# Out projections of a one-core decoder layer: weight high parts against both parts of the activations in one 512-column matmul, two accumulators per tile, residual added two tiles at a time

## The reference

```
x = x + 0.5*g1 * ((silu(h@Wa) * (h@Wb)) @ w_ffn1_out)      # h = mod(rms(x)), D_FF = 5504
P = h @ w_in ; SSD mixer, S5 mixer ; merged = sig(ga)*(y_a@w_a) + sig(gb)*glu(y_b@w_b)
x = x + g2 * (merged @ w_out)                               # 2048 x 2048
x = x + 0.5*g3 * ((silu(h@Wa) * (h@Wb)) @ w_ffn2_out)
out = rms(x)*norm_final
```

## The kernel before, in words

| stage | phase | k tiles, k tiles per slab | ada slabs per body | after it |
|---|---|---|---|---|
| A | first FFN, out, first rows | 20: 4,4,3,3,3,3 | 4 | "in" stage |
| B | first FFN, out, last rows | 23: 4,4,4,4,4,3 | 8 | norm |
| C | w_out | 16: 4,4,4,4 | 4 | norm |
| D | second FFN, out, first rows | 20: 4,4,3,3,3,3 | 0 | "in" stage |
| E | second FFN, out, last rows | 23: 4,4,4,4,4,3 | 0 | final norm and output |

## Time and profile before

### The profile page before, as it was taken

How to read it: one execution, slowest core, us unless ns; L and a number is a source line. 1 busy time by engine, 2 the same in 40 slices (tenths; PEclk the granted TensorE clock), 3 DMA queues, 4 the chain that set the end, 5 groups by cost and what they waited for, 6 DMA issues and landing times. The chain is left out here.

```text
span 2542.8 us, 39831 instructions
## 1 busy us (share of the span) xinstructions
PE 2418.9 (95%) x16288; PEld 2200.0 (87%) x16288; DVE 1728.5 (68%) x2035; ACT 1034.6 (41%) x1109; POOL 222.5 (9%) x250
## 2 busy tenths in 40 slices
PE   5899999999999998889999979989999999999998
PEld 3478799887899998889999979989788899888998
DVE  3357877778778779798777767657767455444554
ACT  3233343333443454444444433433434344434443
POOL 2500413132133000000000000000000000000000
PEclk8899999999999999999999989999999999999999
DMA  9967777878877865454566658567678556655652
GB/s 332 360 244 275 267 272 259 302 256 297 273 263 269 308 233 166 158 190 167 166 209 215 213 177 281 181 212 269 233 248 308 185 183 199 194 187 176 195 176 99
DMA packets 296990, 584.58 MB, mean 230 GB/s; under 512 B 10324, under 2 KB 35412, under 8 KB 295316
## 3 DMA queue, kind: packets, MB, share of 16 engines
q1 hardware_dynamic: 291408, 559.98, 64.6%
q0 software_dynamic: 4144, 22.28, 2.5%
q10 hardware_dynamic: 1300, 0.35, 0.1%
HBM read 569.98 MB, written 12.58 MB: 229 GB/s over the span
## 5 line engine op out<-in xcount | busy, mean ns | idle before, releaser
L900 DVE TENSOR_TENSOR wlo<-raw,whi 128x1024 fp32r<-128x1024 f32 x800 | 984.6, 1272 | 591.4 <-ACT whi L524 580.2
L524 ACT ACTIVATE whi<-raw 128x1024 fp32r<-128x1024 f32 x800 | 803.6, 1052 | 1237.1 <-PE gps L296 1185.3
L296 PE MATMUL gps<-whi,hs 128*128 128x512 f32 (+1 forms) x2816 | 874.9, 389 | 25.1 <-DVE wlo L900 18.0
L296 PE MATMUL gps<-hs,whi 128*128 128x256 f32 x3584 | 662.9, 287 | 36.6 <-DVE hs L1448 14.9
L296 PEld LDWEIGHTS gps<-whi,hs 128*128 128x128 f32 x2816 | 532.0, 190 | 134.5 <-DVE wlo L900 22.4
L296 PEld LDWEIGHTS gps<-hs,whi 128*128 128x128 f32 x3584 | 564.2, 194 | 49.2 <-issue 29.0
L296 PE MATMUL gps<-wlo,hs 128*128 128x512 f32 (+1 forms) x1408 | 545.0, 387 | 0.0
L296 PE MATMUL gps<-hs,wlo 128*128 128x256 f32 x1792 | 509.8, 284 | 0.0
L296 PE MATMUL gps<-ffs,whi 128*128 128x256 f32 x2752 | 498.9, 284 | 5.3 <-DVE wlo L900 5.3
L296 PEld LDWEIGHTS gps<-ffs,whi 128*128 128x128 f32 x2752 | 429.1, 192 | 7.3 <-DVE wlo L900 6.9
L296 PE MATMUL gps<-ffs,wlo 128*128 128x256 f32 x1376 | 389.3, 283 | 0.0
(11 more groups left out here) (251 smaller groups left out, 1231.6 us busy)
## 6 DMA issues: line engine op xcount, KB each, us to landing
raw<-in_w_ffn_in_dram SPq DMA_DIRECT2D x160, 1024.0 KB
raw<-in_w_ada_dram SPq DMA_DIRECT2D x112, 1024.0 KB
raw<-in_w_in_dram SPq DMA_DIRECT2D x80, 1024.0 KB
raw<-in_w_ffn_out_dram SPq DMA_DIRECT2D x56, 1024.0 KB
pre<-in_w_ada_dram SPq DMA_DIRECT2D x32, 1024.0 KB, 13.8
raw<-in_w_ffn_out_dram SPq DMA_DIRECT2D x40, 768.0 KB
raw<-in_w_a_proj_dram SPq DMA_DIRECT2D x16, 1024.0 KB
raw<-in_w_b_glu_dram SPq DMA_DIRECT2D x32, 512.0 KB
```

The source lines that it names most:

```text
L296: return pe.matmul(out, lhsT, rhs, start=start, stop=stop, skip_group_check=True)
L524: act.activation(whi[:, mpos % SPLIT, h, :], raw[:, pos % RING, h, :], ACT.Copy).then_inc(hi_ready, 1)
L900: ins = dve.tensor_tensor(wlo[:, mpos % SPLIT, h, :], raw[:, pos % RING, h, :], whi[:, mpos % SPLIT, h, :].bitcast(F32), ALU.subtract)
```

## The change

In the five stages a tile j now has a whole bank: `wps` is the same memory as `gps` seen as four tiles of two 256-column accumulators. The weight's high part is multiplied with high and low activations in one matmul of 512 columns (both accumulators), the low part with the high activations in one of 256 columns (first accumulator). So three matmuls (768 columns, three weight loads) become two (768 columns, two weight loads). A group uses all four banks, so a group's first matmuls of tiles 0 and 2 wait until VectorE has read tiles 0,1 and 2,3 of the group before. VectorE adds each tile in two operations, the second after the first; tiles 0,1 as soon as the new `tiles_done` says so, tiles 2,3 when the group is done. The place in its queue moves up: right after the first slab of the next group (before: after the first two). The loops over bodies are written out on VectorE.

```diff
         gps = ctx.enter_context(nc.psum_tensor("gps", [P, 2, 4, S], F32))
         mps = ctx.enter_context(nc.psum_tensor("mps", [P, 4, 512], F32))
+        wps = gps[:, :, :, :].rearrange("p b (h w) s -> p (b h) w s", w=2)
...
             def squares(ph, n, q):
-                act.wait_ge(psum_free(n % 2), q)
+                act.wait_ge(psum_free(1), q)
...
                 elif ph.evac == "resid":
-                    ends = ph.norm is not None and 2 * i + g == 3
+                    n = 2 * i + g
+                    ends = ph.norm is not None and n == 3
+                    gate = hg[:, ph.gate, :]
+
+                    def add(j, part):
+                        t = 4 * n + j
+                        xt = xT[:, t, :]
+                        return dve.scalar_tensor_tensor(out=xt, in0=wps[:, j, part, :], scalar=gate[:, t:t + 1],
+                                                        in1=xt, op0=ALU.mult, op1=ALU.add)
+
+                    def add_both(tiles, count):
+                        for j in tiles:
+                            ins = add(j, 0)
+                        ins.then_inc(sem("x_step"), 1)
+                        dve.wait_ge(sem("x_step"), r.x + 2 * n + count)
+                        return [add(j, 1) for j in tiles]
+
+                    dve.wait_ge(sem("tiles_done"), r.t + n + 1)
+                    xs = add_both((0, 1), 1)
...
+                    xs[1].then_inc(psum_free(0), 1)
+                    if ends:
+                        dve.wait_ge(sem("tiles_done"), r.t + n + 2)
+                        add_both((2,), 2)[0].then_inc(sem("x_new"), 1)
+                        dve.wait_ge(slab_done, m_end)
+                        add_both((3,), 3)[0].then_inc(psum_free(1), 1)
                     else:
                         dve.wait_ge(slab_done, m_end)
-                    gate = hg[:, ph.gate, :]
-                    for j in range(4):
...
-                        ins = dve.scalar_tensor_tensor(out=xt, in0=out[:, j, :], scalar=gate[:, bass.ds(t, 1)],
-                                                       in1=xt, op0=ALU.mult, op1=ALU.add)
...
+                        add_both((2, 3), 2)[1].then_inc(psum_free(1), 1)
...
                                 next(side, None)
+                                if ph.wide and gg == 1 and s == 0:
+                                    evacuate(ph, i, 0, m0 + i * mper + ph.slabs, 0)
                         if g == 1:
...
+                            elif ph.wide:
+                                between = lambda: evacuate(ph, i, 1, m_end, 0)
...
+                def slab_wide(g, i, s, mp, k0):
+                    for j in range(4):
+                        if s == 0 and j % 2 == 0:
+                            pe.wait_ge(psum_free(j // 2), r.q + 2 * i + g)
+                        for k in range(ph.chunks[s]):
+                            hi = whi[:, mp % SPLIT, k, P * j:P * j + P]
+                            lo = wlo[:, mp % SPLIT, k, P * j:P * j + P]
+                            both = moving[:, k0 + k, :, :].rearrange("p w s -> p (w s)")
+                            mm(pe, wps[:, j, :, :].rearrange("p w s -> p (w s)"), hi, both, k0 + k == 0, False)
+                            ins = mm(pe, wps[:, j, 0, :], lo, moving[:, k0 + k, 0, :], False,
+                                     k0 + k == sum(ph.chunks) - 1)
+                        yield ins
...
-                                if ph.norm is not None and 2 * i + g == 3 and s == ph.slabs - 1 and j == 1:
-                                    ins.then_inc(sem("half_done"), 1)
+                                if ph.wide and s == ph.slabs - 1 and (
+                                        j == 1 or j == 2 and ph.ends and 2 * i + g == 3):
+                                    ins.then_inc(sem("tiles_done"), 1)
```

More of the change, by code:

```diff
@@ L85, in __init__ @@
         assert len(self.stream) % RING == 0 and n % SPLIT == 0
+        self.wide = evac == "resid"
+        self.rounds = (2 if self.wide else 1) * bodies
+        self.ends = 1 if norm is not None else 0
 def plan():
@@ L610, in evacuate @@
                     if ph.norm is not None and 2 * i + g == 3:
-                        last_squares(ph, q)
+                        last_squares(ph, r.q + 4)
                     return
@@ L703, in gemm @@
                 body(ph.bodies - 1, following)
-                r.q += ph.bodies
+                r.q += ph.rounds
                 r.p += {"pair": ph.bodies, "glu": 2 * ph.bodies}.get(ph.evac, 0)
@@ L951, in first_two @@
                     if s == 1 and between is not None:
-                        multiply(*between)
+                        between()
                     if i is None:
@@ L1010, in evacuate @@
-                    ins.then_inc(psum_free(b), 1)
+                        add_both((2, 3), 2)[1].then_inc(psum_free(1), 1)
                     if ph.norm == 3:
+                        for b in range(2):
+                            dve.wait_ge(psum_free(b), r.q + n + 1)
                         if ends:
-                            dve.wait_ge(sem("x_new"), 9)
-                        dve.wait_ge(psum_free(b), q)
+                            dve.wait_ge(sem("x_new"), 6)
                         for j in range(4):
-                            t = 8 * i + 4 * g + j
+                            t = 4 * n + j
@@ L1071, in body @@
                                 next(side, None)
+                                if ph.wide and gg == 1 and s == 0:
+                                    evacuate(ph, i, 0, m0 + i * mper + ph.slabs, 0)
                         if g == 1:
-                            between = (ph, m0 + i * mper + 2 * ph.slabs, r.q + i + 1) if ph.evac == "pair" else None
+                            m_end, between = m0 + i * mper + 2 * ph.slabs, None
+                            if ph.evac == "pair":
+                                between = lambda: multiply(ph, m_end, r.q + i + 1)
+                            elif ph.wide:
+                                between = lambda: evacuate(ph, i, 1, m_end, 0)
                             if nxt == "loop":
@@ L1082, in body @@
                                     pass
-                        evacuate(ph, i, g, m0 + i * mper + (g + 1) * ph.slabs, r.q + i + 1)
+                        if not ph.wide or g == 1 and (nxt is None or nxt != "loop" and ph.norm is not None):
+                            evacuate(ph, i, g, m0 + i * mper + (g + 1) * ph.slabs, r.q + i + 1)
                     if ph.ada:
                         ada_end(r.c + i * ph.ada + ph.ada - 1)
-                if ph.bodies > 1 and not ph.side and ph.norm is None:
+                if ph.bodies > 1 and not ph.side and not ph.wide:
                     if after_norm:
@@ L1095, in gemm @@
                 body(ph.bodies - 1, following)
-                r.q += ph.bodies
+                r.q += ph.rounds
+                if ph.wide:
+                    r.t, r.x = r.t + 4 + ph.ends, r.x + 8 + ph.ends
                 r.c += ph.ada * ph.bodies
@@ L1228, in early @@
             def early(ph, following):
-                first_two(following, between=(ph, 8, 1))
+                first_two(following, between=lambda: multiply(ph, 8, 1))
                 evacuate(ph, 0, 1, 8, 1)
@@ L1675, in body @@
                             pass
-                        else:
+                        elif not ph.wide:
                             pe.wait_ge(psum_free(g), r.q + i)
@@ L1686, in body @@
                                 pe.wait_ge(sem("prod_free"), ff_from[0] + (k0 + ph.chunks[s] + 3) // 4 + 1)
-                            if by_tile:
+                            if ph.wide:
+                                parts = slab_wide(g, i, s, mp, k0)
+                            elif by_tile:
                                 parts = (slab_pair_by_tile if ph.evac == "pair" else slab_plain_by_tile)(g, s, mp, k0)
```

18 lines of the change are left out of this document (6 added, 12 removed).

## The result

| | before | changed |
|---|---|---|
| median of the runs (6 and 6) | 2544.4 us | 2554.9 us |
| lowest to highest | 2543.8 to 2545.9 | 2553.5 to 2562.8 |
| profiled execution: time, span | 2544.55, 2542.8 | 2554.86, 2553.1 |
| ratio of times, 95% interval | | 1.0046 (1.0036 to 1.0057) |

What follows compares the result with a forecast made beforehand. TensorE was taken as the busy engine in all five stages, wholly in C, D and E. A 21.8 us gain against 29.9 of new waits gave +8.1, a median of 2553.6 us, range 2541 to 2561.

Steps and rivals of the forecast that it cites:

- What it removes: All five stages: three matmuls become two, a pair takes 0.3467 us for 0.3600; 1632 pairs save 21.8 us.
- its own sign: Stretches without waits: a pair starts every 0.347 us; the prediction is wrong if not within 0.345 to 0.349.
- its bounds: Time of a pair: 0.333 us if the removed weight load takes both fixed parts, 0.360 if nothing is gained.
- Waits at group ends: Ends of groups in A, B, D, E: TensorE waits for VectorE's adds behind a low part, typically losing 1.43 us.
- VectorE's queue: Doubled adds delay ada slabs and low parts, so TensorE waits: C 3.8, A 3.4, B 1.2 us; 8.4 together.
- the rival that these chains vanish: VectorE's chain is cheaper than counted; if its three terms vanish the sum is -0.3 us; chance 0.26.
- Ends of stages: Last adds of B, C and E finish later, by 2.2, 0.1 and 0.9 us.
- B's sum: Stage B: -4.9 saved, +2.9, +1.3, +1.2 and +2.2 added, net +2.7 us.
- the third rival: A cascade in A and B: waits delay low parts further or B's norm pause costs clock; +4 to +12 us; chance 0.06.
- The other side: One weight load less hides more: a pair below 0.3417 us makes the kernel faster, 2532 at the bound; chance 0.12.
- The one with no gain from merging: The pair costs what three matmuls cost, 0.36 us: +29.9, 2575.5 us; chance 0.03.

Runs made afterwards that it cites:

- narrow_two: The changed kernel with only the merging undone: three 256-column matmuls per tile and k tile, its layout, adds and waits kept; 2565.9 us, ratio 1.0086.
- last4: The changed kernel with slab sizes reordered so the last slab of each FFN output group has four k tiles, not three; 2545.9 us, ratio 1.0009.
- one_part: The changed kernel without the second accumulator's adds and without VectorE's wait for itself between the two adds; 2537.7 us, ratio 0.9977.
- the control: The kernel before with two slab-size tables reordered so the last slab has four k tiles; 2547.7 us, ratio 1.0016.
- ada_later: The changed kernel with the four ada slabs of each body in stage A one weight slab later; 2551.4 us, ratio 1.0029.
- grouped: The changed kernel with each tile's 512-column matmuls in a slab placed ahead of its 256-column ones; 2554.5 us, ratio 1.0043.
- orders: The changed kernel with four different orders of the 512- and 256-column matmuls tried in the groups of D and E; 2554.2 us.
- slab_runs: The changed kernel with all 12 or 16 512-column matmuls of a slab in D first, except in a group's last slab; 2552.7 us.

## Why the prediction was right, and where it was not

The table takes each stage to the first matmul of what follows (for E, to the end of the span). "Saved" after is 0.360 less the stage's mean pace, times its pairs; "added" is the net plus that.

| | saved, forecast / measured | added | net |
|---|---|---|---|
| A | 4.3 / 2.5 | 7.5 / 6.4 | +3.2 / +3.9 |
| B | 4.9 / 4.4 | 7.6 / 8.9 | +2.7 / +4.4 |
| C | 3.4 / 2.4 | 3.9 / 3.3 | +0.5 / +1.0 |
| D | 4.3 / 3.2 | 5.7 / 5.6 | +1.4 / +2.4 |
| E | 4.9 / 3.7 | 5.2 / 4.6 | +0.3 / +0.9 |
| sum | 21.8 / 16.2 | 29.9 / 28.8 | +8.1 / +12.6 |

The profiled execution is 10.3 us longer. The rest of the program took 2.3 us less in it than in the profile of before, 1.8 of that between B's norm and C; that was not followed further, and no term of the forecast covers it. So part of the nearness is luck: in its own five stages the forecast was 4.5 us short.

- **What it removes: this step failed, by its own sign.** "A pair in a stretch without waits starts every 0.347 us", wrong if not within 0.345 to 0.349. It is 0.3467 in some stretches and 0.3533 in others, 0.3501 on average: 9.9 ns saved for each removed matmul, not 13.3, 16.2 us for 21.8. I added the paces of two uniform streams; mixed, they cost up to half of the saving again. The text did say that no row shows them alternating, and 0.350 lies between its bounds. By the Trainium skill ("TensorE: Matmul & The Clock Gate", section "Wait — 56ns, not 53.3ns?") the fixed part of back-to-back matmuls is about 2.5 ns, and the removal would have been worth an estimated 4.1 us. The trace does not agree: 16.2 us by the paces, and narrow_two 11.0 in the whole.
- **Waits at group ends: right** in cause and number, and in D and E in size: seven waits of 1.15 to 1.24 us idle, which is 1.39 in full where it was followed, for 1.43. last4 and one_part confirm the cause there from both sides. The other seven vary: idle 1.16 and 1.09 in mid body of A, 0.45 and 0.28 at its body ends (about 0.7 and 0.5 in full, for 0.6), 0.74 at the body end of B (1.0 for 1.3), and 1.24 and 2.10 in mid body of B (1.5 and 2.3, for 1.43 each). The 15.4 us and 0.23 for each of 14 restarts make 18.6, forecast 18.3.
- **VectorE's queue: right in kind, somewhat too large.** In C two low-part waits, 2.6 us idle in all, about 3.1 with the restarts, for 3.8. In A eight waits with 5.2 idle for the five with 3.3 before, 2.7 more with the restarts, for 3.4. In B none more: one of 1.9 for two with 2.0 together before, where the sum had 1.2. That is 5 to 6 us of the 8.4 forecast, so the rival that these chains vanish is refuted, but a third of them did not come. A slower pair gives VectorE more time, so the two errors lean against each other; narrow_two shows this in A.
- **Ends of stages.** B 1.5 us for 2.2 (its norm begins 8.7 after the last residual matmul for 7.2), E 0.2 for 0.9. Both too high.
- **B's sum was too small**, +4.4 for +2.7, with one item that I had put under the third rival, at 0.06: the clock, 3.4 us. It is in the next but one section.
- **The rivals.** The other side needed a pair below 0.3417, and no stretch shows one. The one with no gain from merging needed 0.360.

## To carry to other kernels

Fewer, wider matmuls save only the fixed part, here 9.9 ns each, and they are paid for in accumulators: ask how many banks the next group then shares with this one, and what stands in the queue of the engine that empties them, between the last matmul and the release. In D and E the wait was removed by a table of slab sizes, not by a faster engine: there the slab during which the next weights are split has to last longer than the copy, the split and the four adds that release the first banks. And run the kernel before with such a side edit too: it was the control that kept 3.4 us of the table in A from being booked on the change.

## What the runs showed of the hardware that I had not expected

**Mixed widths.** The 20 ns for each round trip between 256 and 512 columns, and the two exact paces of an alternating stream, 0.3467 and 0.3533, held over as many as 316 pairs (D in last4 behind its first four, at 0.3533).

**The clock in stage B.** The windows view of the same stretches, first of the change, then of the kernel before (the clock is the third column from the right):

```profile
785.00:800.00 15.00, 13.11 (x65) 11.01 (x65) 14.76 (x15) 3.25 (x4) 4.44 (x3) 0.89 0.89 296
840.00:850.00 10.00, 7.90 (x37) 6.57 (x36) 6.32 (x11) 2.00 (x2) 0.00 (x0) 0.83 0.90 315
```

```profile
785.00:800.00 15.00, 14.68 (x123) 14.47 (x122) 14.64 (x17) 4.02 (x4) 1.05 (x2) 1.00 0.87 304
840.00:850.00 10.00, 10.00 (x86) 10.00 (x85) 5.07 (x10) 4.54 (x5) 0.00 (x0) 1.00 0.81 295
```

The granted clock fell to 1.2 GHz twice for 3.4 us. The first time, at 788.8, TensorE had waited 1.89 us for a low part, until 787.74; the second time, at 843.4, it had waited 2.10 us for the adds, until 842.57. A pair then takes 0.64 us; at half pace 3.4 us cost 1.7, so 3.4 us in B in all. The kernel before had a wait of 1.70 at nearly the same place and kept 2.4 GHz. The forecast had taken from the earlier trace rows that waits between slabs do not lower the clock; here they did. The length of the one wait does not tell when: in last4 the same wait of 1.89 passed without a fall, and the clock fell at 810.0, just behind one of 1.43. one_part shows a fall in A too, at 416.3, at the end of a wait of 2.52. Of the 14 profiles, the eight with the change in B (the changed kernel, last4, one_part, ada_later, narrow_two, grouped, orders, slab_runs) all show one or two such falls in B, each near the end of a wait of 1.4 to 2.1 us, and the six without it none. In six of them a fall comes at 803 to 810 us, at the body end of B. That the falls follow from the change in B is so far shown; what it takes besides a wait is not, since no run tests it by itself.
